# First blocks of the second input projection fetched and split inside the output projection before it; the last SSD group's output weights and convolution rows handled after the next step's decays

## What is computed

```python
def retention_layer(h, s0, pos, w_in, head_norm, w_out):
    ...
    return (o * jax.nn.silu(gate)) @ w_out, s_new

def ssd_layer_full(h, s0, conv0, w_in, conv_w, conv_b, dt_bias, a_log, d_skip, gate_norm, w_out):
    proj = h @ w_in                                   # second input projection
    z, xbc, dt_raw = ...
    xpad = jnp.concatenate([conv0, xbc], axis=1)
    conv = conv_b
    for w in range(SSM_CONV):
        conv = conv + xpad[:, w:w + L] * conv_w[w]
    xbc_c = jax.nn.silu(conv)
    new_conv = xpad[:, L:]                            # rows that are given back
    ...
    y, s_new = chunked_linear_recurrence(cm, bm, v, log_a, s0)   # chunks of 128 tokens
    y = (y + xs * d_skip[:, None]).reshape(b, L, SSM_DINNER)
    g = _rms((y * jax.nn.silu(z)).reshape(b, L, SSM_GROUPS, -1)) * gate_norm
    return g @ w_out, s_new, new_conv
```

## Time and profile before

| | us |
|---|---|
| three executions | 2179.25, 2180.72, 2184.92 |
| their median | 2180.72 |
| the profiled execution, its own time | 2190.38 |
| its span in the trace | 2188.6 |

### The profile page before, as it was taken

The page is one execution under the profiler, slowest core; times in us unless marked ns, Lnnn a source line. Parts: engine busy times, 40 slices in busy tenths (PEclk is TensorE's granted clock), DMA queues, the critical chain, the costliest instruction groups (busy, mean ns, idle before and its releaser), DMA issues. The chain is left out here.

```text
span 2188.6 us, 40782 instructions
## 1 busy us (share of the span) xinstructions
PE 2049.3 (94%) x14070; PEld 1892.8 (86%) x14070; DVE 1307.8 (60%) x1929; ACT 889.3 (41%) x1947; POOL 394.0 (18%) x558
## 2 busy tenths in 40 slices
PE   6999999999899998999689999999999999977998
PEld 6999999999677776788589999999999999965787
DVE  7755899766455575222244757575767676665322
ACT  7222121332444454232344545454545545455431
POOL 0200000000222220000001424342433333340000
PEclk9999999999999998999799999999999999978999
DMA  4433333334779895343512333333332333275341
GB/s 131 136 103 101 99 91 109 115 95 128 217 256 283 285 313 196 96 139 102 166 26 76 82 81 93 91 81 86 82 91 79 86 91 81 65 228 140 116 137 39
DMA packets 387153, 274.12 MB, mean 125 GB/s; under 512 B 117713, under 2 KB 342705, under 8 KB 386921
## 3 DMA queue, kind: packets, MB, share of 16 engines
q1 hardware_dynamic: 338806, 242.77, 37.9%
q10 hardware_dynamic: 48144, 28.76, 4.3%
HBM read 184.59 MB, written 86.88 MB: 124 GB/s over the span
## 5 line engine op out<-in xcount | busy, mean ns | idle before, releaser
L1581 PE MATMUL p3acc_ps<-xn2hi,p3whi 128*128 128x272 f32 x1536 | 463.6, 302 | 21.5 <-DVE xn2lo L2293 15.3
L1581 PE MATMUL p3acc_ps<-xn2lo,p3whi 128*128 128x272 f32 x1536 | 447.8, 292 | 0.0
L1581 PE MATMUL p3acc_ps<-xn2hi,p3wlo 128*128 128x272 f32 x1536 | 447.5, 291 | 0.0
L269 PE MATMUL p1ps<-x1hi,w1hi 128*128 128x272 f32 x1288 | 373.0, 290 | 4.7 <-issue 3.1
L269 PE MATMUL p1ps<-x1hi,w1lo 128*128 128x272 f32 x1288 | 372.8, 289 | 0.0
L269 PE MATMUL p1ps<-x1lo,w1hi 128*128 128x272 f32 x1288 | 371.8, 289 | 0.0
L1581 PEld LDWEIGHTS p3acc_ps<-xn2hi,p3whi 128*128 128x128 f32 x1536 | 294.5, 192 | 23.1 <-DVE xn2lo L2293 15.7
L1581 PEld LDWEIGHTS p3acc_ps<-xn2lo,p3whi 128*128 128x128 f32 x1536 | 294.8, 192 | 0.2
L1581 PEld LDWEIGHTS p3acc_ps<-xn2hi,p3wlo 128*128 128x128 f32 x1536 | 294.1, 191 | 0.0
L269 PEld LDWEIGHTS p1ps<-x1hi,w1hi 128*128 128x128 f32 x1288 | 243.3, 189 | 5.0 <-issue 5.0
L269 PEld LDWEIGHTS p1ps<-x1hi,w1lo 128*128 128x128 f32 x1288 | 243.7, 189 | 0.0
(11 more groups left out here) (323 smaller groups left out, 4385.8 us busy)
## 6 DMA issues: line engine op xcount, KB each, us to landing
w1raw<-in_ret_w_in SPq DMA_DIRECT2D x48, 512.0 KB, 5.0
p3raw<-in_ssm_w_in SPq DMA_DIRECT2D x48, 512.0 KB, 4.6
ret_vg<-y1out SPq DMA_DIRECT2D x32, 512.0 KB, 3.2
r_vg<-ret_vg SPq DMA_DIRECT2D x32, 512.0 KB, 5.3
r_sin<-in_state_ret SPq DMA_DIRECT2D x32, 512.0 KB, 6.4
out_ret_sample<-r_sout ACTq DMA_DIRECT2D x32, 512.0 KB, 6.5
s_cr<-sums SPq DMA_DIRECT2D x64, 256.0 KB, 3.3
ret_qk<-y1out SPq DMA_DIRECT2D x16, 512.0 KB, 3.7
```

Of the source, the lines that this page charges most:

```text
L269: last = nc.tensor.matmul(bank[:, 2 * at + i, 0:HB], w[s][:, idx, k, :], x[:, idx, k, i * HB:(i + 1) * HB], start=(k == 0 and j == 0), sto ...
L1581: last = nc.tensor.matmul(pr_ps[:, n % 2, 0:TB], wt[:, j % 2, k, :], x[:, k, b * TB:(b + 1) * TB], start=(k == 0 and i == 0), stop=(k == K ...
```

## The change

It has two parts.

**First block.** A new helper, `first_block_of`, places the buffers of the SSD stage's first block before the first mix stage starts, and phase_mix p2 gets it as `block_next`. While that stage is at its last tile, SP loads block 0 of `xn2T`, then, when PE is half through the last tile's products, weight slice 0, block 1 and weight slice 1. ACT splits weight slice 0 and block 0 before it handles the last tile, DVE takes their low parts around its own work on the last tile. The wait of SP for its last stores moves from the end of the mix stage to the head of SP's program in the SSD stage. The raw buffers of blocks 0 and 2 change places.

**Last group.** On ACT the weight split and the copy and stores of the convolution rows of step c move from the end of step c to step c+1, behind that step's decays and sums. On DVE the low part of a weight slice moves from behind the output of a step to ahead of the multiplication of decays and scores in the same step.

```diff
@@ phase_mix, SP @@
+                    if block_next is not None and t == NT - 2:
+                        sp.wait_ge(lo_done, part(NT - 1, PARTS - 1))
+                        for i in range(2):
+                            dma_wait(sp, x_out[i], 3)
+                        block_next.load_x(sp, 0)
+                        sp.wait_ge(block_next.spent, 1)
+                        block_next.load_raw(sp, 0, 2 * INNER)
+                        block_next.load_x(sp, 1)
+                        block_next.load_raw(sp, 1, 2 * INNER + SG * SDS)
                     store(t)
...
+                    if block_next is not None:
+                        block_next.unfinished += [(h_out[s], n), (x_out[s], n)]
+                    else:
+                        if h_dram is not None:
+                            dma_wait(sp, h_out[s], n)
+                        dma_wait(sp, x_out[s], n)
@@ phase_mix, PE @@
                         if i == PARTS - 1:
                             last.then_inc(mm, 1)
+                        elif block_next is not None and t == NT - 1 and i:
+                            last.then_inc(block_next.spent, 1)
@@ phase_mix, ACT @@
+                    if block_next is not None and t == NT - 1:
+                        block_next.weights_high(act)
+                        block_next.block_high(act)
                     act.wait_ge(added, t + 1)
@@ phase_mix, DVE @@
+                    last_one = block_next is not None and t == NT - 1
+                    if last_one:
+                        block_next.weights_low(dve)
...
+                    if last_one:
+                        block_next.block_low(dve, 0)
                     dve.wait_ge(root, t + 1)
...
+                    if last_one:
+                        block_next.block_low(dve, 1)
@@ first_block_of @@
+    def weights_high(act):
+        dma_wait(act, raw_in[0], 1)
+        act.wait_ge(spent, 1)
+        nc.scalar.activation(whi[:, 0, :, :], raw[:, 0, :, :], ACT.Copy).then_inc(w_hi, 1)
+
+    def weights_low(dve):
+        dve.wait_ge(w_hi, 1)
+        dve.wait_ge(spent, 2)
+        nc.vector.tensor_tensor(wlo[:, 0, :, :], raw[:, 0, :, :], whi[:, 0, :, :], ALU.subtract).then_inc(w_lo, 1)
+
+    def block_high(act):
+        dma_wait(act, x_in[0], 1)
+        act.wait_ge(spent, 2)
+        for i in range(2):
+            ks = slice(i * KD // 2, (i + 1) * KD // 2)
+            nc.scalar.activation(hi[:, ks, 0:TB], xraw[0][:, ks, :], ACT.Copy).then_inc(x_high, 1)
@@ phase_ssd, SP @@
-                load_raw(0)
-                load_x(0)
-                load_raw(1)
+                for done, n in block0.unfinished:
+                    dma_wait(sp, done, n)
+                block0.load_x(sp, 2)
...
-                load_x(1)
-                load_x(2)
-                load_x(3)
+                block0.load_x(sp, 3)
@@ phase_ssd, ACT @@
+                def conv_rows_out(c):
+                    act.wait_ge(tails_turned, c + 1)
+                    if c:
+                        dma_wait(act, tails_stored, 2 * c)
+                    nc.scalar.activation(tail_rows[:, :], pr_ps[0:CTAIL, 0, :], ACT.Copy).then_inc(tails_taken, 1)
+                    act.wait_ge(tails_taken, c + 1)
...
+                        if c and not more:
+                            if c <= KI - LATE4:
+                                weights.high(act, c - 1)
+                            conv_rows_out(c - 1)
...
-                weights_high(0, 0)
-                block_high(0)
                 weights_high(0, 1)
@@ phase_ssd, DVE @@
+                        if 1 < c <= KI - LATE4 + 1 and not more:
+                            weights.low(dve, c - 2)
                         if following:
                             decay_scores(g1, c1, dec[:, c1 % 2, :, :])
...
-                        if 1 < c <= KI - LATE4 + 1 and not more:
-                            weights.low(dve, c - 2)
...
-                weights_low(0, 0)
-                block_low(0)
                 weights_low(0, 1)
```

More of the change, by code:

```diff
@@ L1350, in phase_ssd @@
         dt_ps, tk, c_ps, tot_ps = bank[:, 2:6, :], bank[:, 0:2, :], bank[:, 5, :], bank[:, 0, :]
-        xraw = [zb[1].rearrange("p j t -> p (j t)")[:, b * KD * TB:(b + 1) * KD * TB] if b < BLK - 1 else
-                zb[0][:, ZS:NT6, :].rearrange("p j t -> p (j t)")[:, 0:KD * TB] for b in range(BLK)]
-        xraw = [x.rearrange("p (k t) -> p k t", k=KD) for x in xraw]
-        x_in = [sem(f"d_x_in{b}") for b in range(BLK)]
-        x_high, x_low, c_in, c_turned, c_taken, d_loaded, d_high, d_low, mm, step, clamped, tr, trd, sums, rows_out = (
-            sem("d_" + x) for x in ("x_high", "x_low", "c_in", "c_turned", "c_taken", "loaded", "high", "low", "mm", "step",
+        xraw, x_in, x_high, x_low = block0.xraw, block0.x_in, block0.x_high, block0.x_low
+        c_in, c_turned, c_taken, d_loaded, d_high, d_low, mm, step, clamped, tr, trd, sums, rows_out = (
+            sem("d_" + x) for x in ("c_in", "c_turned", "c_taken", "loaded", "high", "low", "mm", "step",
                                     "clamped", "tr", "trd", "sums", "rows_out"))
@@ L2445, in split_weights, with first_block_of, load_x, load_raw @@
     return parts
+class FirstBlock:
+    pass
+def first_block_of(nc, sb, A, xn_dram):
+    NX = SHG * SHD // P
+    NT6, ZS = 2 + 2 * NX, 2 + NX
+    with ExitStack() as c:
+        sb(c, "room_keep", [P, (2 * (NCH + 1) + NCH + DB) * SHEADS + CONVDIM // P * CROWS + KI + 8], F32)
+        hi, lo = sb(c, "xn2hi", [P, KD, T], F32R), sb(c, "xn2lo", [P, KD, T], F32R)
+        raw, whi, wlo = sb(c, "p3raw", [P, 2, KD, P], F32), sb(c, "p3whi", [P, 2, KD, P], F32R), sb(c, "p3wlo", [P, 2, KD, P], F32R)
+        mid, th = sb(c, "p3mid", [P, 2, CINW], F32), sb(c, "p3th", [P, CINW], F32)
+        zb = sb(c, "p3zb0", [P, NT6, CINW], F32), sb(c, "p3zb1", [P, NT6, CINW], F32)
+    places = [zb[1].rearrange("p j t -> p (j t)")[:, i * KD * TB:(i + 1) * KD * TB] for i in (1, 2, 0)]
+    places.append(zb[0][:, ZS:NT6, :].rearrange("p j t -> p (j t)")[:, 0:KD * TB])
+    xraw = [x.rearrange("p (k t) -> p k t", k=KD) for x in places]
+    w_v = A["ssm_w_in"][0, :, :].rearrange("(k p) n -> p k n", p=P)
+    x_in = [nc.alloc_semaphore(name=f"d_x_in{b}") for b in range(BLK)]
+    raw_in = [nc.alloc_semaphore(name=f"s_raw{j}") for j in range(2)]
+    x_high, x_low, w_hi, w_lo, spent = (nc.alloc_semaphore(name=x) for x in ("d_x_high", "d_x_low", "s_w_hi", "s_w_lo", "d_spent"))
+    def load_x(sp, b):
+        sp.dma_start(xraw[b], xn_dram.rearrange("(k p) t -> p k t", p=P)[:, :, b * TB:(b + 1) * TB]).then_inc(x_in[b], 16)
+    def load_raw(sp, j, at):
+        sp.dma_start(raw[:, j, :, :], w_v[:, :, at:at + P]).then_inc(raw_in[j], 16)
+    def weights_high(act):
[12 more added lines that the diff above has]
+            nc.scalar.activation(hi[:, ks, 0:TB], xraw[0][:, ks, :], ACT.Copy).then_inc(x_high, 1)
+    def block_low(dve, i):
+        dve.wait_ge(x_high, i + 1)
+        ks = slice(i * KD // 2, (i + 1) * KD // 2)
+        nc.vector.tensor_tensor(lo[:, ks, 0:TB], xraw[0][:, ks, :], hi[:, ks, 0:TB], ALU.subtract).then_inc(x_low, 1)
+    block = FirstBlock()
+    block.shared, block.zb, block.xraw = (hi, lo, raw, whi, wlo, mid, th), zb, xraw
+    block.x_in, block.raw_in, block.x_high, block.x_low, block.w_hi, block.w_lo, block.spent = (
+        x_in, raw_in, x_high, x_low, w_hi, w_lo, spent)
+    block.load_x, block.load_raw, block.weights_high, block.weights_low = load_x, load_raw, weights_high, weights_low
+    block.block_high, block.block_low = block_high, block_low
+    block.sems = x_in + raw_in + [x_high, x_low, w_hi, w_lo, spent]
+    block.unfinished = []
+    return block
@@ L2500, in phase_mix @@
 def phase_mix(nc, sb, ps, sem, tag, A, whi, wlo, NG, scale, eps, eps_g, g_dram, ss_dram, resid, gain, stale, h_dram=None,
-              turned_dram=None, y=None, first=None, weights=None, late=0):
+              turned_dram=None, y=None, first=None, weights=None, late=0, block_next=None):
     NT, PARTS, KP = NCH + 1, 4, KI // 4
@@ L2846, in program @@
                       tokens(A["x_prompt"], A["x_sample"]), A["ssm_norm"][0, :], before, h_dram=h1_dram, turned_dram=xn_dram,
-                      first=next_tile, weights=weights, late=4)
+                      first=next_tile, weights=weights, late=4, block_next=block0)
         release(before)
@@ L2875, in program @@
                     sb(c1, "room_rest", [P, 2 * KD * T + 6 * KD * P + 3 * CINW + zw - 2 * KI * D], F32)
-                    phase_ssd(nc, sb, ps, sem, A, O, shared, xn_dram, params, rows_dram, *steps, g2_dram, ss2_dram, weights, before)
+                    phase_ssd(nc, sb, ps, sem, A, O, block0, xn_dram, params, rows_dram, *steps, g2_dram, ss2_dram, weights, before)
                 release(before)
```

46 lines of the change are left out of this document (16 added, 30 removed).

## The result

| | us |
|---|---|
| the changed kernel, median of 9 runs | 2168.77 (2162.89 to 2175.87) |
| the kernel before, median of 9 runs beside it | 2183.54 (2177.52 to 2191.10) |
| ratio, 95% interval | 0.9931, 0.9916 to 0.9945 |
| the profiled execution of the changed kernel | 2174.62, span 2172.8 |

The account below looks back on a forecast made before the run. PE is busy 94% of the span, so time is won only where it stands still: the passage into the SSD stage (5.0 us) and the last group (7.0). Together 12.0 off the median of 2180.72 gives 2168.7 us, range 2163.5 to 2176.5.

Parts of the forecast that it names:

- Part one: First block, passage into the SSD stage: moved splits cost nothing, stage starts earlier; gain 5.0 us, from 2 to 5.5.
- the 52 increments: PE's queue at the SSD stage's start: they take 7.8 us before anything else, so PE starts at about 1065.5.
- Part two: Last group: weight split, rows' copy and `w4lo` leave the chain; gain 7.0 us, bounds 11 and a loss of 2.
- The middle: Last group's five steps from step 2 to 7: 4 x 1.6 + 2.1 = 8.5 us gained.
- 0.57 + 0.6 + landing: Last group's period as set by ACT waiting for the rows' stores to land: landing 5.5, period 6.7 us.
- the ring over two steps: Last group, PE turning rows after ACT's copy, then DVE, POOL, ACT: 11.7 to 12.8 us for two periods.
- The collision of `w4lo` and POOL: Last group: with `w4lo` elsewhere the gate product falls from 1.58 to 0.73, and 0.84 us more leave the chain.
- stores bind: Rival, last group: landings grow to 6.5 or 7, period 7.7 to 8.2, in all 5 to 8 off: 2174; chance 0.18.
- neither binds: Rival, last group: neither store nor PE binds, period 6.0, part two gives 10 to 12: 2164.5; chance 0.10.
- increments don't hold PE: Rival, passage into the SSD stage: the whole gap of 13.3 us goes, 13.3 + 7 off: 2160.5; chance 0.03.
- late inputs: Rival, SSD stage's start: input rows or a block come late and PE waits, 2 + 7 off: 2171.7; chance 0.07.
- slower: Rival, last group: ACT waits for the rows' stores ahead of the square; at a landing of 9, 2185; chance 0.04.

Follow-up runs that it names:

- experiment 11: Changed kernel with SP's wait for the landing of the last stores back at the end of the mix stage: median 2173.35 us, ratio 0.9955 to the kernel before.
- experiment 3: Changed kernel with the 52 increments moved from PE's queue to POOL's, those needed first in front: median 2169.24 us, ratio 0.9924 to the kernel before.
- experiment 7: Changed kernel with increments on POOL and the convolution's input rows and identity loaded ahead of SP's wait for the last stores: median 2162.44 us, ratio 0.9892.
- experiment 6: Changed kernel with two PSUM banks for the turned rows and, from step 1 on, state loads ahead of the weight slices: median 2165.29 us, ratio 0.9912.
- experiment 10: The changed kernel itself run and profiled once more, nothing altered: ratio 0.9938 to the kernel before, 13.5 us faster.
- experiment 4: Changed kernel with SP issuing the sample state's load ahead of the three weight slices in the last group: ratio 0.9937 to the kernel before.
- experiment 5: Changed kernel with the last group's turned convolution rows in two PSUM banks in turn: median 2167.03 us, ratio 0.9911 to the kernel before.
- experiment 8: Changed kernel with only `w4lo` put back behind the output on DVE: median 2170.05 us, ratio 0.9921 to the kernel before.
- the parts alone: Two runs: changed kernel with its last group put back, ratio 0.9979; kernel before with only the last group changed, 0.9966; together 12.0 us.

## Why the prediction was right, and where it wasn't

**Part one, 5.0 us.** Right, in size and cause. The stretch gave 4.88 us in the profile and 4.6 timed alone. Its two steps were shown one by one: the stage starts 2.8 us earlier because nobody waits for the landing (experiment 11), and the 52 increments are what is late next (experiments 3 and 7). PE's start was foretold at 1065.5; counted on the time line of before, which stands 1.97 us later at the last scaling, it is 1065.67. That the moved splits cost nothing held too, with 0.57 us to spare on DVE where 0.4 was foretold. That the input rows are not yet late was right with the increments in place: the identity was used 12.5 us after its issue and in experiment 3, where PE stood waiting for it, 8.5 us after, so some 4 us of cover were left. Without the increments it cost 4.4 us of waiting at once.

**Part two, 7.0 us.** Right in size, 6.62 in the profile and 7.4 alone. The middle gave 8.9 us against 8.5, step 1 gave 0.4 against 0.7, the end took 2.7 back against 2.0. But the named bound was the wrong one. The step that failed is the period "0.57 + 0.6 + landing" with a landing of 5.5 us: in the changed kernel no wait of ACT is ended by it; in its repetition one is, by 0.3 us. The landings are just short enough there, some under 5.3 us. With the other limits taken away (experiment 6) this one sets one period: a store issued at 1927.31 held ACT's copy until 1933.46, 6.15 us. The rows show two others. In the short periods it is DVE with 6.03 us of 6.10, where I had 5.9 for its own work and left out that `w4lo` would itself grow by 0.37 us in its new place (experiment 10 shows the same period without that growth). In the long ones it is PE, late by the landing of a state (median 6.5 us from 1905 to 1960, 7.3 in the earlier trace rows) or by the ring over two steps through ACT's copy of the rows. That ring stood in the prediction with 11.7 to 12.8 us for two periods; it measured 13.1 to 13.4, and experiments 4 to 6 show both links, each hiding the other. The average of 6.53 us met my 6.6 because three limits lie within 1 us of each other: luck in part.

**The collision of `w4lo` and POOL.** The gate product fell from 1.58 to 0.73 us as foretold, and the rest of the term went too: `w4lo` met POOL's next two instructions instead. The Trainium skill (SBUF — State Buffer, Who interferes with whom) calls the shared port pair of DVE and GpSimd an exclusive lock, and says that issue order decides who blocks. On the order the trace agrees on both sides: `w4lo`, issued 0.05 us behind `s_vt` of 0.61 us, is longer by 0.37, and the decayed state, issued in the middle of `w4lo`, ends 0.47 us after it. The sizes are a little smaller than if each had stood for the whole of the other's recorded time: 0.19 us less on `w4lo`, 0.14 less on the decayed state. Experiment 8 shows 0.9 us for the group in one pair of profiles, not 0.84 a step.

**The sum.** 12.0 us forecast; 11.5 by the two stretches, 12.0 by the parts alone, 13.5 and 15.1 by the whole. That the median of 2168.77 stands so near the 2168.7 of the forecast is luck: the 12.0 were taken off a median of 2180.72, and beside the changed kernel the one before took 2183.54. The rivals: stores bind, neither binds, increments don't hold PE, late inputs and slower all fell; the third by experiments 3 and 7, the others by the rows above. The chance of "faster" was added up wrong: 0.58 + 0.10 + 0.03 and two thirds of 0.18 + 0.07 are 0.88, not 0.84; the forecast doesn't hang on it.

## What to carry to other kernels

When a gap is to be closed, list everything that ends in it, the increments in an engine's queue too, and order it by time. Here the next limit stood close behind each time: the identity took back 5.5 of 8.2 us (experiment 3), the turned rows all of what the early states gave (experiment 4), and an edit showed its full worth in the profile only with the second link gone as well (experiments 3 and 7, 4 and 6). And compare single profiled executions by stretches between instructions that both kernels have: the untouched ones, and the same code profiled again, tell how much of a difference is chance.

## What was not expected of the hardware

An increment of a semaphore is not free in a row: 52 of them take 7.8 us on PE's queue (0.15 us each, of which the row shows 51 ns as the instruction) and 4.3 us on POOL's (0.083 each, 17 ns). The instructions of that line in experiment 3:

```profile
L2114 POOLq EVENT_SEMAPHORE  x52: 17/17/17, 1054.0 to 1058.3; - x52
```

And the landing of a 128 KB load beside a stream of weights differs from one execution of the same code to the next: the load of a state issued at 1926.70 us took 7.4 us in the changed kernel, and its repetition's, issued at 1926.65, took 8.4. The period that followed was 7.31 us in the one and 8.31 in the other.
